# Column sums for the modulation of a transformer kernel, and its 24 pieces spread over the first three stages

## What is computed

```python
c_act = jax.nn.silu(c)
for i in range(DEPTH):                                # DEPTH = 2
    mod = c_act @ ada_w[i] + ada_b[i]                 # ada_w[i] is 1024 x 6144
    sh1, sc1, g1, sh2, sc2, g2 = jnp.split(mod[:, None, :], 6, axis=-1)
    h = x * (1 + sc1) + sh1
    y = neighbourhood_mixer(h, ...) if i % 2 == 0 else gqa_mixer(h, ...)
    x = layer_norm(DEEPNORM_ALPHA * x + (1 + g1) * y, ln_g[i, 0], ln_b[i, 0])
    h = x * (1 + sc2) + sh2
    y = hierarchical_moe(h, ...)
    x = layer_norm(DEEPNORM_ALPHA * x + (1 + g2) * y, ln_g[i, 1], ln_b[i, 1])
```

## Time and profile before

| what | us |
|---|---|
| median of the runs | 1555.37 |
| lowest and highest of the runs | 1554.26 and 1557.9 |
| span of the profiled execution | 1548.5 |
| PE busy in that span | 1384.9 |
| DVE busy in that span | 563.6 |
| ACT busy in that span | 214.9 |

### The profile page before, as it was taken

The page is one execution under the profiler, slowest core; times in us unless marked ns, Lnnn a source line. Parts: engine busy times, 40 slices in busy tenths (PEclk is TensorE's granted clock), DMA queues, the critical chain, the costliest instruction groups (busy, mean ns, idle before and its releaser), DMA issues.

```text
span 1548.5 us, 28441 instructions
## 1 busy us (share of the span) xinstructions
PE 1384.9 (89%) x12810; PEld 880.9 (57%) x12810; DVE 563.6 (36%) x1254; ACT 214.9 (14%) x574; POOL 88.4 (6%) x95
## 2 busy tenths in 40 slices
PE   7999999999999999879879787879999798798795
PEld 4886478678886556435445343457765363454451
DVE  3696459656753321111111115794111111111113
ACT  2230123012332000000000002442100000000000
POOL 3100111000003000000000001100200000000000
PEclk9999999999999999989989899989999898899898
DMA  9656845767769999999999999357999999999995
GB/s 346 219 192 231 307 163 179 273 241 268 272 274 389 415 426 426 427 427 426 428 425 427 426 379 337 110 202 279 423 409 426 427 427 427 427 426 426 425 418 200
DMA packets 98296, 533.33 MB, mean 344 GB/s; under 512 B 5344, under 2 KB 7584, under 8 KB 74352
## 3 DMA queue, kind: packets, MB, share of 16 engines
q1 hardware_dynamic: 94432, 519.40, 83.2%
q0 software_dynamic: 3728, 11.95, 2.2%
HBM read 530.28 MB, written 1.05 MB: 343 GB/s over the span
## 4 chain that ended last, share of the span: by engine, by line
PE 66%; DMA 26%; DVE 4%; SPq 2%; issue 1%; ACT 1%; DVEq 0%; ACTq 0%
PE bk L438 28%; PE bk L910 17%; DMA ring<-in_moe_w_down 16%; DMA AR<-in_moe_w_down 9%; PE bk L946 8%; PE bk L619 4%; PE bk L956 4%; PE bk L434 2%; SPq L2356 2%; PE bk L648 1%; PE bk L663 1%; DVE AR L1031 1%; ACT AR L1852 1%; DMA ring<-in_w_in 1%; DVE AR L1039 1%
## 5 line engine op out<-in xcount | busy, mean ns | idle before, releaser
L910 PE MATMUL bk<-ring,AR 128*32 128x128 f32 x4480 | 267.7, 409 | 4.4 <-DMA ring<-in_moe_w_up 4.4
L1031 DVE TENSOR_TENSOR AR<-bk,AR 128x128 f32<-128x128 f32 (+2 forms) x106 | 41.3, 390 | 517.4 <-ACT AR L1852 451.5
L910 PEld LDWEIGHTS bk<-ring,AR 128*32 128x32 f32 x4480 | 178.8, 127 | 83.8 <-DMA ring<-in_moe_w_up 6.9
L910 PE MATMUL bk<-AR 128*32 128x128 f32 x3712 | 223.4, 409 | 3.5 <-DMA AR<-in_moe_w_up 2.8
L438 PE MATMUL bk<-ring,AR 128*128 128x256 f32 (+2 forms) x736 | 210.6, 444 | 6.5 <-ACT AR L1852 2.9
L946 PE MATMUL bk<-ring,AR 128*32 128x512 f32 x608 | 158.9, 696 | 51.4 <-DMA ring<-in_moe_w_down 50.6
L1852 ACT ACTIVATE AR<-bk 128x512 f32<-128x512 f32 (+4 forms) x178 | 72.0, 422 | 928.6 <-PE bk L910 757.5
L910 PEld LDWEIGHTS bk<-AR 128*32 128x32 f32 x3712 | 145.0, 127 | 74.1 <-DMA AR<-in_moe_w_up 5.9
L438 PEld LDWEIGHTS bk<-ring,AR 128*128 128x128 f32 x736 | 139.6, 192 | 71.4 <-issue 54.4
L946 PE MATMUL bk<-AR 128*32 128x512 f32 x416 | 149.6, 693 | 29.5 <-DMA AR<-in_moe_w_down 29.5
L438 PE MATMUL bk<-AR,ring 128*128 128x256 f32 (+1 forms) x832 | 170.5, 364 | 1.7 <-DVE AR L1036 1.4
(11 more groups left out here) (154 smaller groups left out, 947.9 us busy)
## 6 DMA issues: line engine op xcount, KB each, us to landing
ring<-in_moe_w_gate SPq DMA_DIRECT2D x36, 2048.0 KB, 28.8
ring<-in_moe_w_up SPq DMA_DIRECT2D x34, 2048.0 KB, 26.4
AR<-in_moe_w_up SPq DMA_DIRECT2D x30, 2048.0 KB, 29.7
AR<-in_moe_w_gate SPq DMA_DIRECT2D x28, 2048.0 KB, 26.8
ring<-in_moe_w_down SPq DMA_DIRECT2D x28, 2048.0 KB, 34.4
ring<-in_ada_w SPq DMA_DIRECT2D x24, 2048.0 KB, 10.8
AR<-in_moe_w_down SPq DMA_DIRECT2D x22, 2048.0 KB, 34.2
ring<-in_w_in SPq DMA_DIRECT2D x12, 2048.0 KB, 12.8
```

Source lines behind the costliest of these rows:

```text
L910: ins = eng.matmul(o[32 * f:32 * f + 32, 128 * m:128 * m + 128], XG[u][:, c, 32 * j:32 * j + 32], w[:, c, f::4], start=c == 0, stop=c == N ...
L1031: return eng.tensor_tensor(o, a, b, op)
```

## The change

**Totals as columns.** Two pieces share one part buffer of 1024 columns (`mpart`, `mpart2`). `total(m)` runs over a pair m: for each of eight interleaved column sets c, the part's columns c, c+8, ... are the stationary operand (128x128) and one column of ones is the moving one, so that the sum stands with its features on the partitions, in eight columns of a bank. `extract(m)` is then one instruction of 128x8 which adds the bias and, for scales and gates, the one. The reductions `dsum` and the four loads of the gates' bias are gone.

**Gates by a diagonal.** DVE's `gate_rows(n)` multiplies the identity with the gate's columns into `diag` or GROW (two TENSOR_TENSOR of 64x512), PE's `gate_rows` makes each half of 512 by one product over 64 rows, and ACT copies two halves of 512 instead of four of 256. `second_gates` is gone; the gates g2 are made in `router` whole.

**The pieces' places.** Pieces 0 to 6 are summed in mix layer 0, 7 to 14 in mix layer 1, 15 to 23 in NA, none in GQA. There are 12 totals, 3 in mix layer 0, 4 in mix layer 1, 5 in NA, where 24 were.

```diff
-LOADS = (("cq", "qk", "v", "ada", "s", "a", "ada", "b", "ada", "g", "ada", 0, "ada", 1, "ada"),
-         ("cq", "ada", "qk", "v", "ada", "s", "a", "ada", "b", "ada", "g", "ada", 0, "ada", 1, "ada"))
+LOADS = (("cq", "qk", "v", "ada", "s", "a", "ada", "b", "ada", "g", "ada", 0, "ada", 1, "ada", "ada"),
+         ("cq", "ada", "qk", "v", "ada", "s", "a", "ada", "b", "ada", "g", "ada", 0, "ada", 1, "ada", "ada"))
...
-NA_SIDE = ((), ("x13", "+", "+"), ("x14", "+", "+"), ("x15", "+", "+"), ("x16", "+", "+"), ("x17", "+", "+"),
-           ("m", "+", "+"), ("l", "o00"), ("o01",), ("o02", "o03", "s"))
...
+NA_SIDE = (("+",), ("x7", "+", "+"), ("x8", "+", "+"), ("+", "+"), ("x9", "+", "+"), ("+", "+"), ("m", "x10", "+"),
+           ("l", "d", "o00"), ("x11", "o01"), ("o02", "o03", "s"))
...
-GQA_SIDE = (("x20", "v10"), ("w10",), ("v01", "+", "w01"), ("+",), ("v11", "+", "w11"), ("+",), ("x21", "n", "+"), ("m", "+", "o00"),
-            ("l", "o01"), ("o02", "x22", "o03", "s"))
+GQA_SIDE = (("v10",), ("w10",), ("v01", "w01"), ("d",), ("v11", "w11"), (), ("n",), ("m", "o00"), ("l", "o01"), ("o02", "o03", "s"))
+GQA_LOADS = ((2, 14), (0, 39), (1, 52), ("wo", 0, 105), ("wo", 1, 113))
...
-            def total(n, b):
-                o = begin(b, "adaT", n)
+            def total(m):
+                o = begin(next_bank(), "adaT", m)
                 pe.wait_ge(sem("ones"), 1)
-                pe.wait_ge(sem("ada"), n + 1)
-                end(product(o[:, :], [(ones[:, :], part(n))]), "adaT", n)
+                pe.wait_ge(sem("ada"), 2 * m + 2)
+                a = PART[m % 2][:, :].rearrange("p (k c) -> p c k", c=NC)
+                for c in range(NC):
+                    ins = eng.matmul(o[:, c:c + 1], a[:, c, :], ones[:, 0:1], start=True, stop=True)
+                end(ins, "adaT", m)
+
+            def gate_rows(n, to, *name):
+                o = [begin(to[h], *name, h) for h in range(2)]
+                pe.wait_ge(sem("ones"), 1)
+                pe.wait_ge(sem("gd"), n + 1)
+                for h in range(2):
+                    r = slice(64 * h, 64 * h + 64)
+                    end(eng.matmul(o[h][:, :], ones[r, :], gate_diagonal(n)[r, :], start=True, stop=True), *name, h)
...
-                        if n > 1:
-                            v.wait_ge(*filled("adaT", n - 2 if n < 15 else n - 4))
+                        if n > 3:
+                            v.wait_ge(*filled("adaT", n // 2 - 2))
...
+            def extract(m):
+                i, k = divmod(m, 6)
+                v.wait_ge(sem("in2"), 16 * (ADA_IN + DEPTH))
+                v.wait_ge(*filled("adaT", m))
+                free(stt(mod[:, i, 8 * k:8 * k + 8], bank("adaT", m)[:, 0:8], 1.0 if k % 3 else 0.0, abc[:, i, 8 * k:8 * k + 8],
+                         ALU.add, ALU.add), "adaT", m)
+
+
+            def gate_rows(n):
+                i, k = n // 2, (2, 5)[n % 2]
...
+                for h in range(2):
+                    r = slice(64 * h, 64 * h + 64)
+                    ins = tt(gate_diagonal(n)[r, :].rearrange("p (k c) -> p k c", c=8), bcast(ident[r, r], 2, 8),
+                             bcast(mod[r, i, 8 * k:8 * k + 8], 1, 64), ALU.mult)
...
-                extract(12)
+                extract(6)
                 norm_columns(0, 0, 3)
-                ada(8)
+                gate_rows(0)
+                ada(24)
                 todo = list(NA_SIDE)
...
-                ada(8)
                 for f in ROPED[0:3]:
```

191 lines of the change are left out of this document (74 added, 117 removed).

## The result

The changed kernel takes 1645.72 us (median of 4 runs, 1640.56 to 1646.9), the kernel before 1556.63: ratio 1.0578, interval 1.055 to 1.0606. It is slower, as forecast, but by 5.8% and not by 3.7%: 1613 was forecast, and 1645.72 lies above the range of 1586 to 1630. The profiled execution has a span of 1643.2 us, 94.7 more than before.

A forecast was written before the change was run, and what follows sets the result against it. PE was taken to bound the second mix stage and NA, DMA the stages from 485 us, neither PE nor DVE alone GQA. 1548.5 + 1 (mix) + 58 (NA) + 7 (clock) - 8.5 (GQA) = 1606, plus 6.9: 1613 us; range 1586 to 1630.

The forecast's parts named there:

- The mix stages: Both mix stages: 7 column totals at 1.78 replace 13 row totals at 0.96, about 0; taken as +1 us.
- D: Rival: each column-total pass costs a whole 0.48, 7.7 a total, +41 in the mix stages, 1653 and more; chance 0.02.
- NA head: Start of NA: late pieces 15 to 18 delay the first mask-add and stall PE before q2, +37 us.
- the walk: Step-by-step tracing on paper: in NA of slots, landings and DVE's work; in GQA of two queues, round by round.
- Second and third stall: Later in NA: PE waits before k4 behind piece 19, +11 us, and before the gates behind piece 23, +8.5.
- Totals in NA: Five column totals in NA: total 7 and total 11 add 0.8 us each, the other three are hidden in stalls.
- Clock: After PE's three idle stalls the granted clock falls, costing 1.3 to 3.4 us each; +7 (4 to 10).
- GQA: Grouped attention: four pieces less on DVE gain 7.2, one total less 0.96, gates 0; together -8.5 us (6 to 11).
- The 6.9 outside the span: Whole program: median of runs 1555.37 against profiled span 1548.5, so 6.9 us was added to the 1606.
- The skill's rule on packing: Gates in GQA: matmuls on different row groups overlap, making GQA's sum -10; left out, no trace row showing such a pair.
- C: Rival: stalls are worse, each late landing at the long end and the clock at +10; 1628 us, chance 0.15.
- B: Rival: NA head pieces come in time or don't hold PE, only PE's own work counts; 1552 us, chance 0.05.

The follow-up runs named there:

- e1_contig: Changed kernel with DVE writing the part in column order (c, k), so each stationary tile of a column total is contiguous; 1643.1 us, ratio 1.0586.
- e10_after_rows: Changed kernel with column totals replaced by row totals, a pair's halves on the two halves of the partitions, same result as the reference; 1615.15 us, ratio 1.0392.
- e4_gqa: Kernel before with pieces 20 to 23 left out of GQA and nothing put elsewhere; 1551.01 us, ratio 0.9977.
- e9_rows: e3_plan with the row totals of e10_after_rows, two to a bank, and gates by a diagonal; 1553.84 us, ratio 0.9991 against the kernel before.
- e8_slots: Changed kernel with other slots and load order in NA, pieces 16 and 17 in the slots of 13 and 14, DVE's order kept; 1628.41 us, ratio 1.0485.
- e3_plan: Changed kernel with NA's pieces placed as before, one at its head, and two pieces back in GQA; 1595.68 us, ratio 1.0267.

## Why the prediction was wrong, point by point

**What bounds.** Right. The shift of the first issue into the extra slots went through the experts' stages with 0.6 us of change (2.3 more, less 1.7 for the gates at their end), and that of the second with 2.3. Where these 2.3 come from was not looked into.

**The mix stages: the step that failed.** "The nearest row is the router's 128x36, also 16 passes ... 1.78". The number of passes and the few moving columns were the same; the stationary operand was not. In the router's product it is contiguous, in the total its columns stand 8 apart. A pass of the total then takes 0.24 instead of 0.11 to 0.12 (3.7 us for 16), as e1_contig showed on PE, where it changes that alone. The prediction did not look for the step; and the one row of before that has it, the transposes of x (16 passes in 2.06), would have given 1.8 to 2.1 a total, which is no better than the 1.78. 7 totals cost 26 us in the place of 12.5 for 13 old ones, 13.5 more. The other 10 us of the 23.7, by difference, are the rows at half speed behind each total, a mechanism that the prediction knew only behind idle time. The bound that I gave with the full pass (0.48) was too high, and no chance in it stood for a price between the two ends: D had it at 0.02. That D's 1653 stands near the measured time is luck; its price of a pass is twice the measured one. The Trainium skill ("TensorE: Matmul & The Clock Gate", "LDWEIGHTS (loading the stationary operand)") has the time follow from the number of columns alone; by it the estimate was 1.7 us a total. The trace agrees for the contiguous operand (1.84 in e1_contig) and not for the strided one (3.68 in the changed kernel): the measurement decides. Another page would have warned me, and I did not weigh it: the Trainium skill, "SBUF — State Buffer", "Door 1: The DMA port swizzle (why `[64,N]` ≈ `[32,N]`)", says that accesses pay when each goes to a new line of 16 bytes, which a step of 32 bytes always does. PE's passes in the totals (0.24 for 0.12) and DVE's sums (1.16 for 0.78) agree with its direction; the transposes of x, with the same step 0.11 a pass, start no further apart for it.

**NA head.** The chain of landings was right. Less the 23.7 of the mix stages, DVE begins pieces 16, 17 and 18 at 341.3, 357.2 and 377.0, where the walk had them landed at 343.5, 358.3 and 378.1. The mask-add started 65.4 later than before; 23.7 of that came in with the mix stages, 41.7 is the stage's own, where the walk had 380.9 against 338.03 and 1 of shift, 41.9. PE's stall was 29.6 and not 37, since PE itself came later to the wait, by a total of 3.83 and slow rows. Second and third stall: 7.15 and 6.04 for 11 and 8.5, likewise. e10_after_rows has all three at 37.24, 12.97 and 11.22. Pieces 20 and 21, which the walk had in DVE's pace, made DVE wait 9.10 and 9.83, but no stall of PE stands behind them.

**Totals in NA.** "The other three are hidden in the stalls" was half wrong: five totals at 3.83 instead of five rows at 0.96 are 14.4. What a total delays ahead of a stall the stall gives back; behind the last stall nothing does.

**Clock.** Forecast 7, and for three places. NA's +73.9 less 42.3 of added stalls (0.45 of them there before) less 14.4 leaves 17, by difference: slow rows behind five totals and three stalls, such as 16.12 for the first projections instead of 14.05, and 10.02 for q2 and q3 instead of 7.

**GQA.** The table's stretch has -5.8. The prediction's -8.5 also counted the gates at the head, which stand in the stretch before; with them it is -7.5, inside the range of 6 to 11, but put together otherwise. The pieces gave less: e4_gqa has 4.4 for them alone. The walk had the rounds follow DVE and left out ScalarE, for which PE waits 1.93 in a round freed. The gates gave 1.7, forecast 0 in the sum: 8 passes over one row took 3.78, 4 passes over 64 rows 2.08, both at 0.50. In the changed kernel, then the same product of g1 in NA of e9_rows, where the clock is 1.00:

```profile
1042.12 2.08 PE L475 MATMUL bk<-diag,ones 64*128 64x512 f32 x4 [4.99 <-issue]
```

```profile
423.55 1.13 PE L476 MATMUL bk<-AR,ones 64*128 64x512 f32 x4 [0.40 <-issue]
```

**The 6.9 outside the span.** The sum added the difference between the median of the runs and the profiled span. Wherever a run has both for one execution they differ by 1.7 to 1.8 us (1645.02 and 1643.2 for the changed kernel). So 5 of the 6.9 were the spread between executions of the kernel before. Against the span, 1606 was forecast and 1643.2 came.

**The skill's rule on packing.** The sentence "No row of this trace shows such a pair" was true of before; the changed kernel has it at the lower clock (1042.12 above) and e9_rows at the full one. There four passes of 64x512 take 1.06 from start to start (423.55 above, the next row at 424.61). One after another they would take 4 times 0.48, the pass of a row total, which is 1.92. The two halves, on rows 0 to 63 and 64 to 127, do overlap, and so do the two halves of e9_rows's total on different columns. So the rule of the Trainium skill ("TensorE: Matmul & The Clock Gate", "Part 3: Packing small matmuls — row/col tiling") agrees with the trace.

**Rivals.** None was the one that came. C had the stalls longer; they were shorter, and the totals were dear. B's turning point, pieces 15 to 18 in time, was not reached by any run: e8_slots has 15 to 17 in time and 18 not, and a stall of 15.78 stays. e3_plan, with one piece at the head, has no stall there.
